# Where VectorE's state updates stand in the recurrence: ahead of the dot rows, rates and scaled operands

## The reference, cut to what matters

```python
def step(S, inp):
    w_t, k_t, v_t, kk_t, a_t = inp[:5]
    sa = jnp.einsum('bhvk,bhk->bhv', S, kk_t)
    S = (S * w_t[:, :, None, :]
         - sa[..., None] * (kk_t * a_t)[:, :, None, :]
         + v_t[..., None] * k_t[:, :, None, :])
    y = jnp.einsum('bhvk,bhk->bhv', S, inp[5]) if emit else None
    return S, y
```

```python
u = jnp.take(p['peer_u'], eidx, axis=0)
act = jax.nn.gelu(jnp.einsum('td,thkd->thk', hc, u).astype(jnp.float32), approximate=False) * gw
v = jnp.take(p['peer_v'], eidx, axis=0)
return jnp.einsum('thk,thkd->td', act.astype(hc.dtype), v)
```

## Time and profile before

| what | value |
|---|---|
| three runs | 5067.23, 5072.8, 5088.39 us |
| span of the profiled execution | 5070.9 us |
| TensorE | 3553.5 us busy, 70% |
| VectorE | 2546.2 us busy, 50% |
| GpSimd | 1732.9 us busy, 34% |
| ScalarE | 1029.7 us busy, 20% |
| DMA | 1117.61 MB, 220 GB/s on average |

### The profile page before, as it was taken

One profiled execution on the slowest core, in us unless ns is written; L12 is line 12 of the kernel. 1 busy time (PEld: TensorE's weight loads), 2 busy tenths in 40 slices (PEclk: granted clock), 3 DMA queues, 4 the chain that ended last, 5 costly groups with the idle time before them and its releaser, 6 DMA issues. The chain is left out here.

```text
span 5070.9 us, 86238 instructions
## 1 busy us (share of the span) xinstructions
PE 3553.5 (70%) x35214; PEld 2697.6 (53%) x35214; DVE 2546.2 (50%) x6002; ACT 1029.7 (20%) x2629; POOL 1732.9 (34%) x1745
## 2 busy tenths in 40 slices
PE   7989886986666786655635699887430335977798
PEld 6777774875444563554411387776300001875687
DVE  2846538667666264786650034663869341143310
ACT  1224321222222111332200123442100000112300
POOL 0000001335777345467777300000577775000000
PEclk9999997996888897877767799998765767988899
DMA  5332335877898697678999642003799998311242
GB/s 212 129 113 102 119 108 205 314 240 246 300 319 307 238 344 293 224 251 295 322 373 409 241 145 83 3 3 112 252 387 407 405 403 329 128 50 61 83 165 92
DMA packets 298903, 1117.61 MB, mean 220 GB/s; under 512 B 33680, under 2 KB 39072, under 8 KB 289952
## 3 DMA queue, kind: packets, MB, share of 16 engines
q0 software_dynamic: 221184, 805.40, 43.3%
q1 hardware_dynamic: 77344, 306.90, 17.2%
HBM read 1111.13 MB, written 1.05 MB: 219 GB/s over the span
## 5 line engine op out<-in xcount | busy, mean ns | idle before, releaser
L2113 POOL DMA_INDIRECT ring<-in_peer_u,expert_number x620 | 737.0, 1189 | 1141.7 <-DVE expert_number L2424 566.1
L2070 DVE CUSTOM_DVE_ANT_0 ring<-ring,tok 128x1024 f32<-128x1024 f32 x620 | 749.4, 1223 | 327.1 <-DMA ring<-in_peer_u,expert_number 313.4
L2096 PE MATMUL psum<-spare,picked 128*32 128x512 f32 x1472 | 262.1, 847 | 463.4 <-POOL picked L2147 360.9
L2096 PEld LDWEIGHTS psum<-spare,picked 128*32 128x32 f32 x1472 | 56.1, 135 | 658.9 <-issue 658.9
L177 PE MATMUL psum<-h,weight_ring 128*128 128x256 f32 x1728 | 385.2, 387 | 22.6 <-PEq L96 22.6
L2127 POOL DMA_INDIRECT spare<-in_peer_v,expert_turned x368 | 352.9, 959 | 100.0 <-issue 90.7
L177 PEld LDWEIGHTS psum<-h,weight_ring 128*128 128x128 f32 x1728 | 335.8, 195 | 71.4 <-issue 23.9
L1801 PE MATMUL psum<-h,weight_ring 128*128 128x256 f32 x1344 | 294.4, 380 | 2.9 <-PEq L96 2.9
L1801 PEld LDWEIGHTS psum<-h,weight_ring 128*128 128x128 f32 x1344 | 254.8, 190 | 41.1 <-issue 6.9
L1317 PE MATMUL psum<-h,weight_ring 128*128 128x256 f32 x1056 | 236.2, 385 | 8.7 <-PEq L96 8.7
L1317 PEld LDWEIGHTS psum<-h,weight_ring 128*128 128x128 f32 x1056 | 202.7, 193 | 40.8 <-issue 12.4
(11 more groups left out here) (606 smaller groups left out, 7175.1 us busy)
## 6 DMA issues: line engine op xcount, KB each, us to landing
weight_ring<-in_w_in SPq DMA_DIRECT2D x226, 512.0 KB, 3.5
ring<-in_ada_w SPq DMA_DIRECT2D x24, 1024.0 KB, 11.9
weight_ring<-in_w_q SPq DMA_DIRECT2D x48, 512.0 KB, 3.6
weight_ring<-in_ada_w SPq DMA_DIRECT2D x16, 1024.0 KB, 6.6
weight_ring<-in_w_out SPq DMA_DIRECT2D x32, 512.0 KB, 3.5
gate_ring<-in_w_gate SPq DMA_DIRECT2D x32, 512.0 KB, 3.4
weight_ring<-in_w_mlp_in SPq DMA_DIRECT2D x32, 512.0 KB, 3.4
weight_ring<-in_w_mlp_out SPq DMA_DIRECT2D x8, 2048.0 KB, 8.7
```

What stands on the lines that cost most here:

```text
L2070: dve.tensor_tensor_reduce(place.rows, place.rows, b.tok[:, tile, :], 1.0, 0.0, ALU.mult, ALU.add, b.dots[:, tile, slot:slot + 1]).then_in ...
L2096: mm = pe.matmul(out, place.window.columns[:, strip, first:first + STRIP], part.rows[:, 512 * half:512 * half + 512], start=(m % BATCHES = ...
L2113: pool.indirect_dma_start(place.rows, None, b.tables["u"], bass.IndirectOffsetOnAxis(ap=b.number[:, r:r + 1], axis=0)).then_inc(place.sem, 16)
```

## The change

Only VectorE's order in the state phase changes, and the numbers that keep GpSimd's order. Before the first step, `sums` now comes ahead of the one dot row, not behind it. In each step the four instructions of the state update now come first. Behind the update of step 0 stand two dot rows, the rates and two dot rows, which stood ahead of it. Behind the update of step 1 stand scaled and then four dot rows, where two rows, scaled and two rows stood ahead of it. No instruction is added or removed.

```diff
             dve.wait_ge(k.vec_step.sem, k.vec_step.mark)
-            k.step_of(17)
-            use_rows(k, dve, 1)
             if following is not None:
                 following.sums(dve)
             marks["summed"] = k.vec_step.count
+            k.step_of(17)
+            use_rows(k, dve, 1)
...
             for n in range(2):
-                k.step_of(18 + 2 * n)
-                use_rows(k, dve, 2)
-                if following is not None:
-                    (following.scaled if n else following.rates)(dve)
-                use_rows(k, dve, 2)
                 for i in range(2):
...
                     marks["S", n, i] = k.vec_step.count
+                k.step_of(19 + 2 * n)
+                if following is None:
+                    use_rows(k, dve, 4)
+                elif n == 0:
+                    use_rows(k, dve, 2)
+                    following.rates(dve)
+                    use_rows(k, dve, 2)
+                else:
+                    following.scaled(dve)
+                    use_rows(k, dve, 4)
```

## The result

The changed kernel takes 5086.22 us (median of eight, 5079.3 to 5094.53) where the kernel before takes 5070.24 (eight): ratio 1.0036, 95% interval 1.0021 to 1.005. I had forecast 5069, four microseconds less than the median shown before; the changed kernel is 16 us slower than the kernel before. The span of the profiled execution is 5090.0 us against 5070.9.

A forecast was written before the change was run, and what follows sets the result against it. Units were taken as bound differently: by TensorE, VectorE or GpSimd; the target was TensorE's 159.6 us wait for VectorE's state. 21 + 5 - 21 - 7 - 2 = -4 us on 5070.9 gave 5067, adjusted to 5069; range 5043 to 5097.

The forecast's parts named there:

- Part 1: 14 units without dot rows, first and fourth recurrence: scaled behind the last update lengthens them, +21 us, bounds 19 to 22.
- Rival C: End of the 14 units without dot rows: TensorE's longer gap lowers the clock, +20 us, 5089 us; chance 8%.
- Part 2: Six units with dot rows alone: waits for a row's gather appear, +5 us, bounds 0 to 12.
- Part 3: Eight units with batches and a next unit: TensorE's step 1 starts sooner, -21 us, bounds 0 and -45.
- Part 4: Last units of recurrences two and three: shorter by 7 and 2.2 us, bounds -4 to -11 together.
- A: Units with batches: transfers have no room, so the eight units gain nothing; +19 us, 5092 us; chance 14%.
- B: Units with batches: GpSimd's waits for dot rows give way too; -30 us, 5043 us; chance 16%.

The follow-up runs named there:

- e5: The kernel before, unchanged, run on a chip where it takes 5309 to 5331 us: ratio 1.0006.
- e13: Changed kernel plus four unused filler matmuls behind the last Y in the 14 units without expert work that have a next one: 5067.82 us, 1.0003 of the kernel before.
- e18: Kernel before with the new order in all units with expert work only: 5049.48 us, 0.9956 of the kernel before.
- e15: Kernel before with the new order only in the ten units with batches: 5052.36 us, 0.9964 of the kernel before.
- e16: Kernel before with only sums and the first update early, in the ten units with batches: 5051.32 us, 0.9961 of the kernel before.
- e17: Kernel before with only the second update and scaled ahead of their four rows, in the ten units with batches: 5091.96 us, 1.0041 of the kernel before.
- e14: Kernel before with three of scaled's four operations repeated behind the last update in 14 units without expert work: 5089.09 us, 1.0039 of the kernel before.

## Why the prediction was wrong

**Part 1** held for what it counted. The path grew by 19.1 us for a forecast of 21 (the state phase, from TensorE's first R to the next unit's L906, went from 14.7 to 16.2 us in each unit of the first recurrence: 1.5 for 1.6; in the fourth 1.1 to 1.3 for 1.4). The claim that its bounds were narrow, "19 to 22", was wrong, because it counted only instructions that run unchanged, and they did not: the matmuls behind the gap ran at the lower level.

**Rival C is what happened, and the clock is the step that failed.** The sum, 21 + 5 - 21 - 7 - 2, has no term for the clock; the 19 us stood beside it as rival C, at 8%. C said +20 us and 5089. The traces show 19.2, the filler gave back 17.9 and the kernel took 5086. I gave C 8% on the ground that units of the first recurrence "hold 1.00 with TensorE idle for 3 us in all". That sum is made of pieces, the longest 1.33 us at the end. The change put its 1.5 us into that very piece, as C's first sentence says and as follows from Part 1, which I held for certain. No row showed what a piece of 2.9 us does, and I took the sum of the pieces in its place.

The unit at 0.95 in the earlier trace rows gave C the right price, 1.4 us for a stretch at the lower level, but not its cause. Its stretch stands in the state phase, some 26 us behind a gap of 1.18 us, where TensorE had waited 0.94 us for ScalarE:

```profile
3202.15 1.11 PE L1133 MATMUL psum<-W,CT 128*64 128x64 f32 x16 [0.94 <-ACT W L1052]
...
3203.81 1.11 PE L1146 MATMUL psum<-W,G 128*64 128x64 f32 x8
```

L1146 takes 0.68 us at the higher level. Each unit of the fourth recurrence has two such waits. One of its first seven units has such a stretch in the kernel before, three have one in e5, and one in e13, whose gaps at the unit's end are 0.56 us. So they do not hang on the gap that C names, and they stay unexplained.

That 5086 lies in my range of 5043 to 5097 is owed to the range's width. That it lies so near C's 5089 is luck in part: Part 4 gave 6 us less than forecast, and the work between the recurrences, where all but one copy stands as before, came out 4.2 us shorter in the pair of traces.

**Part 2** said +5. The first pair of traces has +7.4 and the means of nine have +5.4, with the wait where it was forecast; e18's time does not show it.

**Part 3** was right in size (-19.8 for -21, 18 us in e15) and in its mechanism's first half: the first update early, and the idle time ahead of L2127 down from 4.03 to 0.30 us in the unit followed. Two details were off. The row behind the second update was not waited for, the fifth was. And I let the early second update and the four rows behind it carry part of the gain; e16 has the gain in time without them, and e17 shows a loss of some 21 us when they stand alone.

**Part 4** was mis-sized: -2.6 for -9 (-2.7 in the second recurrence and +0.1 in the third). In the last unit of the second recurrence the update and R did come some 8 us sooner from the unit's start. But then TensorE stood 3.88 us for the parts of its batch:

```profile
1650.50 1.23 DVE L2075 CUSTOM_DVE_ANT_0 ring<-ring,tok 128x1024 f32<-128x1024 f32 x1 [5.89 <-DMA ring<-in_peer_u,expert_number]
...
1652.18 0.69 PE L1110 MATMUL psum<-S,KR 64*64 64x64 f32 x8 [1.79 <-DVE S L1069]
...
1659.69 1.07 PE L2101 MATMUL psum<-x_tokens,picked 128*32 128x512 f32 x2 [3.88 <-DMA weight_ring<-in_peer_v,expert_turned]
...
1664.00 0.90 DVE L1069 SCALAR_TENSOR_TENSOR state<-psum,pc,Sp 128x64 f32<-128x64 f32 x4 [4.39 <-PE psum L1138]
```

The chain of 7.1 us in the earlier trace rows had the parts of its batch landed, since it began 8 us later. Moved up, it took 11.8 us. The last part's gather stands in GpSimd's order behind that of a dot row, which waits for a row to be used; so it went out at 1653.25 us, 41.2 us into the unit, where it had been 43.7: only 2.5 us sooner. In the third recurrence the second update came 6.1 us sooner, but the four rows behind it, two of them waited for, gave that back.

Rivals A and B did not come: GpSimd's waits for dot rows grew, and the transfers had room (315 and 329 GB/s in the units with batches of the second and third recurrence, for 305 and 314).

## What to carry to other kernels

TensorE's idle time at the end of a stage had a price of its own here, in the clock granted behind it: list the longest single gap of each stage, not their sum, and ask of a change whether it makes that gap longer, even where the work is off that engine. Early results for a waiting engine pay only if something is left to do until it answers: move an update up, and keep the independent work behind it. Where the kinds of stage differ, make the change where it pays: the same order cost 38 us in the units without expert work, some 5 in those with dot rows alone, and won 20 in those with batches. The kernel with it in the latter alone is 0.36% faster than the one before, on chips where that takes 5070 us.

## What the runs showed of the hardware

- In the first recurrence, gaps of TensorE of 1.19 to 1.33 us between two stages left the granted clock at 1.00. Gaps of 1.96 to 2.49 us brought a stretch at the 1.2 GHz level behind four of seven (e14), and 2.70 to 2.89 us behind six of seven, with some 1.5 us lost each.
- Four matmuls a unit whose product nobody reads, 2 us in all, gave 17.9 us back over 14 gaps.
- Chips differ by 5% on this program (5070 against 5309 to 5331 us). The units without gathers of the second table take nearly the same on both kinds (the six with dot rows alone 352.6 and 354.2 us). A change that wins 0.4% on the one kind wins nothing on the other.
